# Router sums taken in fp32 from the residual, and the split of the normed chunks spread over the first expert tiles

## The reference, cut to what matters

```python
x = x + g1 * token_mixer(...)                       # its last step is a product with w_out
h = rmsnorm(x, norm2_g) * (1 + sc2) + sh2
aff = sigmoid(h @ router_w)                         # 16 experts in 4 groups
# per token: best group by aff + bias, two experts of it, their weights normalised
x = x + g2 * sum_e combine[:, e] * ((silu(h @ w_gate[e]) * (h @ w_up[e])) @ w_down[e])
return rmsnorm(x, final_g)
```

## Time and profile before

| | us |
|---|---|
| median of three runs | 2849.55 |
| profiled execution, its own time | 2848.54 |
| its span from first to last instruction | 2846.7 |
| TensorE busy | 2792.0 (98%) |
| VectorE busy | 2205.7 (77%) |
| ScalarE busy | 1517.6 (53%) |
| mean granted TensorE clock, share of full speed | 0.993 |

### The profile page before, as it was taken

The page is one execution under the profiler, slowest core; times in us unless marked ns, Lnnn a source line. Parts: engine busy times, 40 slices in busy tenths (PEclk is TensorE's granted clock), DMA queues, the critical chain, the costliest instruction groups (busy, mean ns, idle before and its releaser), DMA issues.

```text
span 2846.7 us, 44159 instructions
## 1 busy us (share of the span) xinstructions
PE 2792.0 (98%) x17174; PEld 2486.7 (87%) x17174; DVE 2205.7 (77%) x2765; ACT 1517.6 (53%) x1741; POOL 158.6 (6%) x227
## 2 busy tenths in 40 slices
PE   8999999999999999999999999999999999999998
PEld 8888888888888989999999989999898888788886
DVE  5775458999886899999999875555765777788887
ACT  5544564445555544444444454555544555566666
POOL 4000010100101000000000020111110000000000
PEclk9999999999999999999999999999999999999999
DMA  7574545555555588888788738444315777789895
GB/s 304 226 301 171 179 153 180 189 192 188 179 195 204 226 336 329 328 324 321 310 324 326 273 121 308 175 162 162 134 57 207 258 296 274 280 303 347 332 350 219
DMA packets 116251, 693.22 MB, mean 244 GB/s; under 512 B 14304, under 2 KB 27856, under 8 KB 35344
## 3 DMA queue, kind: packets, MB, share of 16 engines
q1 hardware_dynamic: 110384, 675.33, 63.1%
q10 hardware_dynamic: 4688, 11.01, 1.2%
q0 software_dynamic: 1040, 4.98, 0.5%
HBM read 680.79 MB, written 10.49 MB: 243 GB/s over the span
## 4 chain that ended last, share of the span: by engine, by line
PE 84%; DVE 8%; ACT 4%; issue 3%; DMA 2%; SPq 0%; DVEq 0%; ACTq 0%
PE psT L1393 12%; PE psT L1380 10%; PE psT L1367 6%; PE psT L1368 6%; PE psT L1369 6%; PE psT L1398 6%; PE psT L1381 5%; DVE w_lo L2227 4%; PE psT L1510 3%; ACT w_hi L672 2%; PE psT L2004 2%; PE psT L2006 2%; PE psT L2005 2%; PE psT L1512 1%; DMA raw<-tiles_dram 1%
## 5 line engine op out<-in xcount | busy, mean ns | idle before, releaser
L2227 DVE TENSOR_TENSOR w_lo<-raw,w_hi 128x2048 fp32r<-128x2048 f32 x531 | 1216.1, 2297 | 332.3 <-ACT w_hi L672 329.0
L672 ACT ACTIVATE w_hi<-raw 128x2048 fp32r<-128x2048 f32 x531 | 1011.3, 1910 | 367.9 <-PE psT L1369 124.5
L1380 PE MATMUL psT<-a_both,w_hi 128*128 128x512 f32 x1440 | 508.5, 398 | 3.4 <-issue 2.6
L1393 PE MATMUL psT<-a_both,w_hi 128*128 128x512 f32 x1504 | 472.8, 396 | 0.8 <-DVE pool L2563 0.8
L1381 PE MATMUL psT<-a_both,w_lo 128*128 128x256 f32 x1440 | 401.7, 279 | 0.0
L1398 PEld LDWEIGHTS psT<-a_both,w_lo 128*128 128x128 f32 x1504 | 282.5, 188 | 66.8
L1380 PEld LDWEIGHTS psT<-a_both,w_hi 128*128 128x128 f32 x1440 | 270.9, 188 | 67.2 <-issue 4.5
L1398 PE MATMUL psT<-a_both,w_lo 128*128 128x256 f32 x1504 | 295.4, 278 | 0.0
L1381 PEld LDWEIGHTS psT<-a_both,w_lo 128*128 128x128 f32 x1440 | 271.9, 189 | 0.3
L1367 PE MATMUL psT<-a_both,w_hi 128*128 128x256 f32 x784 | 228.8, 292 | 8.6 <-DVE pool L2388 3.2
L1393 PEld LDWEIGHTS psT<-a_both,w_hi 128*128 128x128 f32 x1504 | 229.1, 189 | 1.2 <-issue 1.1
(11 more groups left out here) (462 smaller groups left out, 5137.3 us busy)
## 6 DMA issues: line engine op xcount, KB each, us to landing
raw<-tiles_dram SPq DMA_DIRECT2D x531, 1024.0 KB, 5.1
pool<-ada_tiles_dram SPq DMA_DIRECT2D x96, 1024.0 KB, 4.9
bias_rows_dram<-pool ACTq DMA_DIRECT2D x1, 8192.0 KB, 56.1
pool<-bias_rows_dram SPq DMA_DIRECT2D x40, 128.0 KB, 4.4
raw<-tiles_dram SPq DMA_DIRECT2D x12, 256.0 KB, 8.1
pool<-bias_rows_dram SPq DMA_DIRECT2D x40, 64.0 KB, 4.6
pool<-mem_dram SPq DMA_DIRECT2D x4, 512.0 KB, 8.5
pool<-x_dram ACTq DMA_DIRECT2D x1, 2048.0 KB, 11.4
```

Of the source, the lines that this page charges most:

```text
L672: nc.scalar.activation(w_hi[:, t.k % SPL, :], raw[:, t.k % RAW, :], ACT.Copy).then_inc(hi_done, 1)
L1380: nc.tensor.matmul(dst.rearrange("p (h s) -> p h s", h=2), wh, a_both[:, :, a, :], start=first, stop=False)
L1393: nc.tensor.matmul(dst, w_hi[:, t.k % SPL, k * P:k * P + P], a_both[:, :, (k + at) % DC, :], start=k == 0, stop=False)
L2227: nc.vector.tensor_tensor(w_lo[:, t.k % SPL, :], raw[:, t.k % RAW, :], w_hi[:, t.k % SPL, :].bitcast(F32), ALU.subtract).then_inc(lo_done, 1)
```

## The change

- The router's weights are multiplied by `scale2` (`router_parts` on VectorE, behind the tile before the last), the logits are taken as 16 fp32 products from the unnormed residual H, partly ahead of the sums of squares, and are then multiplied by rstd; the shift's part comes in as the sigmoid's bias.
- The adds of the last output tile start when half of it is done (`half_out`), and ScalarE's order at the tail changes: squares first.
- The gained chunks go to PRE2 (slot 16) in place of PRE (slot 0).
- VectorE scales four pairs and finishes two ahead of the choice, a third inside it, and the others between group numbers and expert pieces; the second half of the choice moves behind the third tile's `lo`.
- The second expert tile is split in four pieces too, and two token turns each follow the first and the second tile.
- The turned permutations move from ahead of the first tile to behind the third.

The diff, cut to its core:

```diff
 # ScalarE
+            hi_shifted("norm2", PRE2, mod[:, 48:64], range(4))
+            act.wait_ge(W["logits_scaled"], 1)
+            nc.scalar.activation(pool[0:NE, RSIG, :], flat(RSCALED, 1)[0:NE, :], ACT.Sigmoid, bias=shift_col).then_inc(W["router_sigmoid"], 1)
+            hi_shifted("norm2", PRE2, mod[:, 48:64], range(4, 8))
+            token_copies(range(2))
+            hi_shifted("norm2", PRE2, mod[:, 48:64], range(8, 12))
+            token_copies(range(2, 4))
+            def expert_tile_hi(k):
...
+                for p in range(4):
...
+                    nc.scalar.activation(w_hi[:, t.k % SPL, 512 * p:512 * p + 512],
+                                         raw[:, t.k % RAW, 512 * p:512 * p + 512],
+                                         ACT.Copy).then_inc(W["expert_hi"] if p < 3 else hi_done, 1)
+                    if k == 0 and p % 2:
+                        hi_shifted("norm2", PRE2, mod[:, 48:64], range(11 + p, 13 + p))
+
+            expert_tile_hi(0)
+            token_copies(range(4, 6))
+            expert_tile_hi(1)
+            token_copies(range(6, 8))
+            for k in range(2, AHEAD):
                 split(Tile(BASE["moe"] + k))
             act.wait_ge(W["perms_turned"], 1)
 # TensorE
-            run_sums("norm2")
-            idle_products(20)
-            pe.wait_ge(W["router_lo"], 1)
-            pe.wait_ge(W["variance_ready"], NORM_AT["norm2"] + 1)
+            def logits(part):
+
+                for c in part:
...
+                    last = nc.tensor.matmul(psL, router_rows[:, NE * c:NE * c + NE], pool[:, H + c, :],
+                                            start=c == 0, stop=c == DC - 1)
+                return last
+
+            pe.wait_ge(W["router_ready"], 1)
+            nc.tensor.matmul(psR, shift_part, ones[:, 0:1], start=True, stop=True).then_inc(W["router_sums"], 1)
+            logits(range(1))
+            run_lane("norm2", LANE)
+            logits(range(1, 2))
+            for c in range(4):
+                run_last("norm2", c, SQ)
+            logits(range(2, DC)).then_inc(W["router_sums"], 1)
...
-            for b in range(4):
-                last = narrow(NE, "norm2", range(4 * b, 4 * b + 4))
...
+            idle_products(3)
             pe.wait_ge(W["router_sigmoid"], 1)
             narrow_turned(NE, RSIG).then_inc(W["router_turned"], 1)
+            for n in range(2):
+                turned_tokens(n)
...
+            group_counts()
+            idle_products(8)
+            for n in range(2, 4):
                 turned_tokens(n)
...
+            idle_products(8)
+
+            def turned_perms():
+
+                pe.wait_ge(W["perms_ready"], 1)
...
-            pe.wait_ge(W["tokens_copied"], 8)
             for stage, e in STAGES[:-1]:
                 s, j = EXPERTS[e]
                 if stage == "gate":
                     for k in range(4):
                         expert_part(e, 0, k)
+                        if e == 0 and k < 2:
+                            for n in range(4 + 2 * k, 6 + 2 * k):
+                                turned_tokens(n)
+                        if k == 2 and e == 0:
+                            turned_perms()
 # VectorE
                 if kind == "out":
-                    dve.wait_ge(used, t.count())
+                    final_tile = n == len(SECOND) - 1
+                    if final_tile:
+                        dve.wait_ge(W["half_out"], 1)
...
+                if n == len(SECOND) - 2:
+                    router_parts()
...
-            by_pairs("norm2", PRE, rstd[:, :], bias=mod[:, 48:64])
...
+            pair_scaled(0)
+            pair_scaled(1)
+            pair_lo(0)
+            pair_scaled(2)
+            dve.wait_ge(W["router_sums"], 2)
+            nc.vector.tensor_tensor(flat(RSCALED, 1)[0:NE, :], psL, rstd[0:NE, :], ALU.mult).then_inc(W["logits_scaled"], 1)
+            pair_lo(1)
+            pair_scaled(3)
             dve.wait_ge(W["router_turned"], 1)
...
+            pair_lo(2)
             dve.wait_ge(W["group_counts"], 1)
...
             link(nc.vector.tensor_copy(gid, idx_big[:, 0:4]))
+            pair_scaled(4)
+            pair_lo(3)
+            pair_scaled(5)
+            pair_lo(4)
+            expert_tile_lo(0, range(2))
+            pair_scaled(6)
+            pair_lo(5)
+            expert_tile_lo(0, range(2, 4))
+            pair_scaled(7)
+            pair_lo(6)
+            pair_lo(7)
+            expert_tile_lo(1, range(4))
+            lo(Tile(BASE["moe"] + 2))
```

More of the change, by code:

```diff
@@ L770, in hi_pairs, with hi_shifted @@
                     nc.scalar.activation(a_hi[:, c:c + 2, :], chunks(src + c, 2), ACT.Copy).then_inc(W["act_hi_ready"], 2)
-            def hi_shifted(name, src, bias):
-                for c in range(DC):
+            def hi_shifted(name, src, bias, part=range(DC)):
+                for c in part:
                     pair_waits(name, c)
@@ L1167, in _ @@
                     group_squares("norm2", g, H, SQ)
-                for c in range(4 * g, 4 * g + 4):
-                    if g == 3:
+                if g == 3:
+                    for c in range(12, 16):
                         if c < 15:
@@ L1174, in _ @@
                         last_square("norm2", c - 12, H, SQ)
-                    nc.scalar.activation(pool[:, PRE + c, :], pool[:, H + c, :], ACT.Identity, bias=zero,
-                                         scale=scale2[:, c:c + 1]).then_inc(W["pre_ready"], 1)
+                        if c == 13:
+                            gained(12)
+                            gained(13)
+                    gained(14)
+                    gained(15)
+                    continue
+                for c in range(4 * g, 4 * g + 4):
+                    gained(c)
@@ L1184, in _ @@
[L1184 to L1197, removed]
@@ L1198, in _, with token_copies @@
-            for k in range(1, AHEAD):
+            def token_copies(part):
+                for n in part:
+                    act.wait_ge(W["tokens_turned"], n + 1)
+                    nc.scalar.activation(flat(XT + 8 * (n % 2) + 2 * (n // 2), 2),
+                                         psT[:, 1, 512 * (n % 2):512 * (n % 2) + 512], ACT.Copy)\
+                        .then_inc(W["tokens_copied"], 1)
+            hi_shifted("norm2", PRE2, mod[:, 48:64], range(4))
+            act.wait_ge(W["logits_scaled"], 1)
@@ L1856, in second_half @@
                                          4 * c + k, k == 0, k == 3)
+                    if n == len(SECOND) - 1 and half == 0:
+                        last.then_inc(W["half_out"], 1)
                 else:
@@ L2844, in _ @@
                 if kind == "out":
-                    dve.wait_ge(used, t.count())
+                    final_tile = n == len(SECOND) - 1
+                    if final_tile:
+                        dve.wait_ge(W["half_out"], 1)
+                    else:
+                        dve.wait_ge(used, t.count())
                     dve.wait_ge(W["carried"], 16)
                     for c in range(4 * x, 4 * x + 4):
+                        if final_tile and c == 14:
+                            dve.wait_ge(used, t.count())
                         h = pool[:, H + c, :]
@@ L2879, in _, with pair_scaled, pair_lo @@
                 attend(SECOND_UNITS, 20, SC2, Q2, ticks_at(n, 1, N_UNITS + 4))
-            dve.wait_ge(W["router_hi"], 1)
-            nc.vector.tensor_tensor(hl[:, 0:256], flat(RRAW, 1)[:, 0:256], hh[:, 0:256], ALU.subtract)\
-                .then_inc(W["router_lo"], 1)
+            dve.wait_ge(W["router_sums"], 1)
+            nc.vector.tensor_copy(shift_col, psR)
             root("norm2", D)
             dve.wait_ge(W["pre_ready"], 32)
-            by_pairs("norm2", PRE, rstd[:, :], bias=mod[:, 48:64])
+            rows = rstd[:, :]
+            def pair_scaled(p):
+                pair = chunks(PRE2 + 2 * p, 2)
+                nc.vector.tensor_tensor(pair, pair, rows.unsqueeze(1).to_broadcast([P, 2, S]), ALU.mult)\
+                    .then_inc(W["normed_pairs"], 1)
+            def pair_lo(p):
+                act_lo("norm2", PRE2, 0, bias=mod[:, 48:64], part=range(2 * p, 2 * p + 2))
+            pair_scaled(0)
[6 more added lines that the diff above has]
+            pair_scaled(3)
             dve.wait_ge(W["router_turned"], 1)
```

121 lines of the change are left out of this document (68 added, 53 removed).

## The result

The changed kernel took 2869.8 us (median of four runs, 2867.85 to 2872.63), the kernel before 2850.8 on the same chip: a ratio of 1.0066 [1.0052, 1.0081], that is 18.8 us slower. The forecast was 2861.5 with a range up to 2868, so the sign was right and the time was 1.8 us above the range's top. In a second series, beside thirty runs of the kernel before, the ratio was 1.0042 [1.0027, 1.0057], or 12.0 us. That it is the size forecast to the tenth is luck: its interval reaches from 7.7 to 16.2 us. What sets the two series apart is taken up in the second half of the experiments, and settled there only for the executions that have a profile.

What follows compares the result with a forecast made beforehand. TensorE, busy 98% of the span, bounds the kernel, so an edit only moves its waits. A 6.3 us loss at the mark plus 5.7 of clock dips made 12.0 us slower: 2861.5 us, range 2854 to 2868.

Steps and rivals of the forecast that it cites:

- second tile starts: TensorE starts the second expert tile at 2155.1 us, after a 2.0 us wait; before the change it started at 2162.61.
- wait ahead of second / third / fourth tile: TensorE idles ahead of these expert tiles for 2.0, 4.9 and 5.15 us.
- mark: Start of the first "up" tile: 2179.06 us before the change, forecast at 2185.4 without clock dips.
- The router sums: Router sums ahead of the chunk pairs, 0.43 us per fp32 product, let the choice start 8.25 us earlier.
- rival 2: The router's fp32 sums run slow at doubled price: 18 us slower, 2867.5 us; chance 0.09.
- The order of ScalarE's queue: Copies queued ahead of the third and fourth tiles' rounding make TensorE wait 4.9 and 5.15 us.
- Rival 4: ScalarE reaches third and fourth tiles before the copies, so 7.5 us stay won: 2842 us; chance 0.05.
- The clock: TensorE's clock dips after three tile waits, 1.7 us each, plus 0.6 at the first tile: 5.7 us.
- joint: Stretch from the output projection's last product to the mark, through choice and first expert tiles; forecast 12.0 us longer.
- Rival 1: The clock stays up or dips fall inside the waits: only 6.3 us slower, 2855.9 us; chance 0.17.
- Rival 3: TensorE's 14.5 us idle after 2500 us absorbs the lateness; all 12 would give 2849.5 us; chance 0.07.
- the last of the sum: Adds 12.0 us to the whole kernel's time: 2860.5 us for the profiled execution, 2861.5 for the median.

Runs made afterwards that it cites:

- third_first: Changed kernel with ScalarE rounding the third expert tile ahead of the last two token copies: 2857.77 us, ratio 1.0024 to the kernel before.
- fourth_first: Changed kernel with the fourth tile's rounding and remainder ahead of the copy of the turned permutations: 2853.73 us, ratio 1.0013 to the kernel before.
- the first profile: First profiled execution of the changed kernel, no further edit: 2871.12 us.
- after_again: Changed kernel, unchanged, timed and profiled a second time: 2865.23 us, ratio 1.0042 to the kernel before.
- after_look: Changed kernel, unchanged, run once more for one profile: 2860.91 us.
- after_look2: Changed kernel, unchanged, run for one more profile beside three of the kernel before: 2859.3 us.
- before_look2: Kernel before, unchanged, the second of three further single profiles: 2848.1 us.

## Why the prediction was right, and where it was wrong

| step | forecast, by the clock of before | measured, less 6.37 |
|---|---|---|
| variance | 2127.0 | 2127.2 |
| sigmoid | 2133.5 | 2133.8 |
| choice | 2134.85 | 2135.1 |
| second tile starts | 2155.1 | 2156.6 |
| wait ahead of second / third / fourth tile | 2.0 / 4.9 / 5.15 | 1.93 / 4.81 / 5.16 |
| mark, without the clock's share | 2185.4 | |
| mark | 2191.1 | 2193.4 |

*The router sums.* Right. The 14 fp32 sums took 6.22 us, 0.44 each where 0.43 was taken; rival 2, sums at double the price, is out.

*The order of ScalarE's queue.* Right, place and size: both waits came where they were forecast, within 0.1 us, and each vanished when, and only when, its own tile was moved ahead of the copy (third_first, fourth_first). Rival 4, in which ScalarE gets to the tiles first, is out with them. The Trainium skill, "TensorE: Matmul & The Clock Gate", section "Architectural detail: the array is 16× 32×32, not 1× 128×128", has that engine's queue as strictly first in, first out; the 7.46 and 11.69 us in which ScalarE stood ahead of ready tiles agree.

*The clock.* The mechanism was right, and its terms were nearly so. Forecast were 1.7 us for each of three dips and 0.6 at the first tile, 5.7 in all. Against 5.48 us a tile, the second, third and fourth tile lost 1.72, 1.75 and 3.00 us in the first profile, 0.10, 1.53 and 2.85 in after_again, 1.72, 2.17 and 1.63 in after_look, 1.51, 1.47 and 2.83 in after_look2. Together that is 6.5, 4.5, 5.5 and 5.8 us, where 5.1 was forecast. But for the 0.10, those of the second and third tile are near the row from which they were taken. That of the fourth was 2.8 us or more in three of the four: in the first profile it began inside the wait, at 2187 us, lasted longer than that row's, and reached 6 us into the tile.

The first tile ended 1.45 us late in the first profile, where 0.6 was taken (second tile at 2156.6, not 2155.1; 0.3 of that was the choice). Here the sum missed a third copy of the kind that it found twice. Ahead of the first piece, on ScalarE, stands the copy of the fourth token turn, which TensorE reached behind 16 records of idle products that took 2.58 us. That copy began at 2150.88, and the first piece was rounded at 2151.37, by the clock of before 2145.0 where 2143.5 was forecast. In after_again the same 16 records took 2.03 us, and the first piece began 20.5 us after the last output product instead of 21.8. The next 16 records took 3.17 us in the first profile, and the tile began 0.9 us after its first piece was ready. With the three dips that makes 7.9 us where the sum had 5.7; at the mark the difference is 2.3.

In the four profiles the joint was 11.1 to 14.0 us above the mean of before, so 12.0 lies inside. Rival 1, without dips, would have been a joint of 56.1 + 6.3 = 62.4 us; none of the four was below 67. The Trainium skill, "TensorE: Matmul & The Clock Gate", section "HAM oscillation — how this bites in real kernels", tells of a kernel in which every block behind a wait starts at half rate. The third and fourth tile agree in all four profiles: their first product took 0.79 or 0.80 us, where it takes 0.50 at full clock. The second tile agrees in after_look2 alone; in the first profile and in after_look it began at full clock, which fell within its first 2 us, and in after_again it did not fall.

*Rival 3, absorption.* Out at the size that it needs. TensorE idled less after the mark in the first profile (11.7 us in place of 14.5), so that sign of being wrong did show, but from the mark to the end the four profiles of after took 665.5 to 669.5 us, the five of before 666.4 to 669.5. Means differ by 1.0 us, which is less than the spread of either.

*The step that failed* is the last of the sum: "so 2860.5 for it and 2861.5 for the median". It carried the joint's 12.0 us over to a measurement as if the other 2790 us stood still, and the range was made of the joint's bounds alone. In the profiled execution they did not: 6.4 us came from the pace of the gates, ahead of the joint, 1.9 from behind it, and with the 2.3 by which the first tile and the dips came out longer, and the 12.0 forecast, these are the 22.6. The rows of before could not show a second pace, since that execution had the shorter. Its runs could have warned: three of one kernel spread over 8.6 us, while the range reached 7.5 below the forecast and 6.5 above it. For the other three executions of the first series no profile exists; that they too had the longer pace would fit their times (2867.85 to 2872.63), and is not shown.

## What to carry to other kernels

When work that waits is moved on a queue, list what stands behind it there: a copy of 0.6 or 0.8 us ahead of a ready 1.9 us rounding cost TensorE some 5 us, twice, and putting the rounding ahead gave it all back. After a wait of a few microseconds, add to its price the slower products behind it, here 1.5 to 3.0 us a tile in eleven of twelve cases. And a range for a single measurement needs the spread of executions of the same program as a term of its own, beside the bounds of the change.

## What the runs showed of the hardware that was not expected

- The same instruction stream, with no idle time and at full granted clock, ran at either of two paces: eight tiles in 44.37 or 45.23 us, 394 or 399 ns a product in the mean. One execution can have one pace in an early stage of the gates and the other in a later one: in before_look2 eight tiles took 44.37 us at first, and 45.23 some 60 tiles on.
- A product in fp32 with 16 weight columns on 256 columns took 0.44 us (14 in 6.22), about the price of the mixer's with 128 (0.43 to 0.50): the narrower weights made it no cheaper.
- Filling waits of 2 to 5 us with products that nothing reads kept the granted clock at 1.00 and shortened the joint by some 5 us in the one profile of it, though the waits themselves stayed. A wait of 1.93 us without such products was followed by a lower clock in three of four profiles of one kernel, and by 1.00 in the fourth.
